# Seventeen hardware loops of a two-layer diffusion trunk written out as straight code

## The reference, cut to what matters

```python
for l in range(DEPTH):                       # DEPTH = 2
    need_ctx = l < DEPTH - 1
    mod = (sc @ w_mod[l] + b_mod[l]).reshape(B, 1, N_MOD, D)
    h = modulate(rms_norm(x, g_mix[l]), mod[:, :, 0], mod[:, :, 1])
    ...
    # token_mixer: retention, latent attention (MLA), grouped attention (GQA)
    z = (gs[:, :, 0] * (y_ret @ w_ret_o)
         + gs[:, :, 1] * (y_mla @ w_mla_o)
         + gs[:, :, 2] * (y_gqa @ w_gqa_o))
    y = z @ w_out
    x = x + mod[:, :, 2] * y
    h2 = modulate(rms_norm(x, g_ffn[l]), mod[:, :, 3], mod[:, :, 4])
    x = x + mod[:, :, 5] * ((silu(a) * b) @ w_ffn_out[l])   # a, b = split(h2 @ w_ffn_in[l])
return rms_norm(x, g_final)
```

## Time and profile before

| | |
|---|---|
| median of 3 runs | 3332.19 us (3330.65 to 3338.51) |
| the profiled execution's own time | 3329.75 us |
| its span, first to last instruction | 3327.9 us |
| mean granted TensorE clock over the span | 0.981 |
| PE busy | 3141.2 us (94%), 18376 matmuls |
| PEld busy | 2670.4 us (80%) |
| DVE busy | 1489.7 us (45%) |
| ACT busy | 1215.1 us (37%) |
| POOL busy | 399.5 us (12%) |
| DMA | 303.63 MB, mean 91 GB/s |

### The profile page before, as it was taken

The page is one execution under the profiler, slowest core; times in us unless marked ns, Lnnn a source line. Parts: engine busy times, 40 slices in busy tenths (PEclk is TensorE's granted clock), DMA queues, the critical chain, the costliest instruction groups (busy, mean ns, idle before and its releaser), DMA issues.

```text
span 3327.9 us, 46166 instructions
## 1 busy us (share of the span) xinstructions
PE 3141.2 (94%) x18376; PEld 2670.4 (80%) x18376; DVE 1489.7 (45%) x2073; ACT 1215.1 (37%) x1809; POOL 399.5 (12%) x304
## 2 busy tenths in 40 slices
PE   6899999999999999999999988999999999999998
PEld 5788888899888878788888867877788787778886
DVE  5455524445436634422222255554455456443334
ACT  3344433445434422311211234444355445332222
POOL 0011100111102201000100100111011112010101
PEclk9999999999999999999999989999999999999999
DMA  4111142111241243123132242112222232322232
GB/s 178 64 54 58 65 138 73 58 62 58 76 152 63 82 133 133 57 88 127 63 120 95 101 139 68 62 62 89 82 86 67 89 123 82 133 80 97 95 97 100
DMA packets 99807, 303.63 MB, mean 91 GB/s; under 512 B 10960, under 2 KB 23376, under 8 KB 99664
## 3 DMA queue, kind: packets, MB, share of 16 engines
q1 hardware_dynamic: 54720, 190.34, 16.9%
q10 hardware_dynamic: 44944, 111.32, 10.0%
HBM read 271.73 MB, written 29.88 MB: 91 GB/s over the span
## 4 chain that ended last, share of the span: by engine, by line
PE 79%; DVE 8%; issue 6%; ACT 4%; POOL 1%; DMA 1%; ACTq 1%; DVEq 0%; POOLq 0%
PE ps L1517 73%; PE ps L1605 2%; PE ps L1632 1%; DVE wl L980 1%; ACT wh L487 1%; POOL ptl L1499 1%; DVE tmp L985 1%; DVE ptl L1021 1%; DVE mx L1006 1%; DVE tmp L1153 1%; DVE hl L1162 1%; PE ps L1722 0%; PE ps L1575 0%; ACT pth L523 0%; ACT prob L535 0%
## 5 line engine op out<-in xcount | busy, mean ns | idle before, releaser
L1517 PE MATMUL ps<-hh,wh 128*128 128x512 f32 x2768 | 831.4, 360 | 41.3 <-DVE wl L980 20.2
L1517 PE MATMUL ps<-hl,wh 128*128 128x512 f32 x2768 | 813.4, 354 | 0.0
L1517 PE MATMUL ps<-hh,wl 128*128 128x512 f32 x2768 | 812.0, 353 | 0.0
L980 DVE TENSOR_TENSOR wl<-raw,wh 128x1024 fp32r<-128x1024 f32 (+2 forms) x356 | 465.5, 1308 | 523.1 <-ACT wh L487 509.9
L1517 PEld LDWEIGHTS ps<-hh,wh 128*128 128x128 f32 x2768 | 452.7, 190 | 125.0 <-issue 34.9
L1517 PEld LDWEIGHTS ps<-hh,wl 128*128 128x128 f32 x2768 | 452.2, 190 | 76.4
L1517 PEld LDWEIGHTS ps<-hl,wh 128*128 128x128 f32 x2768 | 453.1, 190 | 73.5 <-issue 0.7
L487 ACT ACTIVATE wh<-raw 128x1024 fp32r<-128x1024 f32 (+2 forms) x356 | 362.0, 1018 | 222.2 <-PE ps L1517 187.1
L1517 PE MATMUL ps<-yh,wh 128*128 128x512 f32 (+1 forms) x1296 | 405.9, 367 | 24.4 <-DVE wl L980 11.9
L1517 PE MATMUL ps<-yh,wl 128*128 128x512 f32 (+1 forms) x1296 | 393.9, 358 | 0.0
L1517 PE MATMUL ps<-yl,wh 128*128 128x512 f32 (+1 forms) x1296 | 393.7, 358 | 0.0
(11 more groups left out here) (212 smaller groups left out, 3312.4 us busy)
## 6 DMA issues: line engine op xcount, KB each, us to landing
raw<-in_stream SPq DMA_DIRECT2D x328, 512.0 KB, 3.2
prob<-in_wmod ACTq DMA_DIRECT2D x40, 512.0 KB, 3.2
mraw<-in_wmod ACTq DMA_DIRECT2D x36, 512.0 KB, 3.3
gspill<-prob ACTq DMA_DIRECT2D x32, 384.0 KB, 2.3
tmp<-gspill ACTq DMA_DIRECT2D x24, 384.0 KB, 3.2
early_y<-in_wmod SPq DMA_DIRECT2D x12, 512.0 KB, 14.2
vraw<-gspill ACTq DMA_DIRECT2D x16, 384.0 KB, 4.0
dec<-in_dec ACTq DMA_DIRECT2D x8, 768.0 KB, 4.2
```

The lines of the kernel that those rows point to most:

```text
L980: dve.tensor_tensor(wl[:, s, 0:n], raw[:, s, 0:n], wh[:, s, 0:n].bitcast(F32), ALU.subtract).then_inc(sem("w_lo"), 1)
L1517: ins = pe.matmul(out, lhs[w], rhs[x](cols), start=start and n == 0, stop=stop and n == 2)
```

## The change

Each of the seventeen `Fori` becomes a Python `for` over the same range, so that every turn is emitted with constants for its waits and addresses: five on ACT (merge, ret, two in out, ffn), five on DVE (the same), three on POOL (the sums in out, ret, ffn) and four on PE (merge, ret, out, ffn). The order of the work on each engine, the buffers and the semaphores stay as they are. The helpers `At.v`, `At.half` and `At.chunk` give the same numbers for a constant turn as for a register.

```diff
 merge, ACT
-                    with act.Fori(0 if ph["begun"] else 1, turns - 1) as i:
+                    for i in range(0 if ph["begun"] else 1, turns - 1):
 ret, ACT
-                    with act.Fori(0, turns - 1) as i:
+                    for i in range(0, turns - 1):
 out, ACT (both branches)
-                        with act.Fori(0, turns - 1) as i:
+                        for i in range(0, turns - 1):
 ffn, ACT
-                    with act.Fori(1 if ph["paired"] else 0, turns) as i:
+                    for i in range(1 if ph["paired"] else 0, turns):
 merge, DVE
-                    with dve.Fori(0 if ph["begun"] else 1, turns) as i:
+                    for i in range(0 if ph["begun"] else 1, turns):
 ret, DVE
-                    with dve.Fori(0, turns - 1) as i:
+                    for i in range(0, turns - 1):
 out, DVE (both branches)
-                        with dve.Fori(0, turns) as i:
+                        for i in range(0, turns):
-                        with dve.Fori(0, turns - 1) as i:
+                        for i in range(0, turns - 1):
 ffn, DVE
-                    with dve.Fori(1 if ph["paired"] else 0, turns) as i:
+                    for i in range(1 if ph["paired"] else 0, turns):
 out (sums), POOL
-                    with pool.Fori(0, turns - 1) as i:
+                    for i in range(0, turns - 1):
 ret, POOL; ffn, POOL
-                    with pool.Fori(0, turns) as i:
+                    for i in range(0, turns):
 merge, PE
-                    with pe.Fori(1, turns) as i:
+                    for i in range(1, turns):
 ret, PE; out, PE
-                    with pe.Fori(0, turns) as i:
+                    for i in range(0, turns):
 ffn, PE
-                    with pe.Fori(1 if ph["paired"] else 0, turns) as i:
+                    for i in range(1 if ph["paired"] else 0, turns):
```

## The result

The changed kernel takes 3315.56 us (median of 5 runs, 3310.99 to 3321.72) where the kernel before took 3334.18 us beside it: a ratio of 0.9941, 95% interval 0.9922 to 0.996. It is faster, by about the size that was forecast (3317.8 us). A second measurement gave 0.9961 (0.9947 to 0.9975). The profiled execution took 3310.99 us with a span of 3309.2 us, 18.8 us less than that of before; as will be seen, some of this difference belongs to the single execution and its clock.

The account below looks back on a forecast made before the run. PE, holding 79% of the chain of waits, was taken to bound the kernel; 5.85 + 1.7 + 3.6 + 3.3 = 14.4 us off the profiled 3329.75 gave 3315.3, so 3317.8 us for the median, range 3309 to 3328.

Parts of the forecast that it names:

- The entries: Four merges after the attentions: PE's waits shrink as ACT's table load and register work before the copy go; 5.85 us.
- Rival (1): Merge entries: table loads stay, inserted by a rule that doesn't see one history; 6.5 us missing, 3324.3 us; chance 0.11.
- rival (2): Merge entries: gain given back at the next wait, gate's load or stream late; 5.85 us missing, 3323.7 us; chance 0.10.
- The clock behind the second entry: After the second merge entry: the 3.42 us stretch at granted clock 0.50 goes with the shorter wait; 1.7 us.
- the clock low in new places: Sign that the prediction is wrong: low granted clock where there was none; a like stretch elsewhere would cost 1.7 us.
- Rival (3): Both `z` and the `out` after them: more low-clock stretches go, 1.7 us each; three make 3312.7 us; chance 0.13.
- The turn ends: First layer's feed-forward out loops: eleven turn ends with PE's branch and register work exposed, 0.33 us each; 3.6 us.
- The dependent steps: DVE and ACT chains PE waits for, at `z`, `out` and first merge folds: shorter gaps between dependent instructions; 3.3 us.
- Worth nothing: Retention, `ffn` loops, inner turns of merge and `out`, POOL's loops, SP's loads: no gain; PE's added code packets: 0 taken.
- Rival (4): New straight stretches: PE's code comes late, 1.1 us per packet boundary; all 60 give 3384 us; chance 0.04.

Follow-up runs that it names:

- the early sigmoid: Kernel before, all loops kept, plus a one-column sigmoid behind the last exponential of each attention: ratio 0.9974, 8.7 us less.
- the three parts that leave the entry alone: Kernel before with only PE's out loop written out (0.9986), only ret and ffn loops (0.9998), or merge on DVE, PE and out on ACT, DVE, POOL (0.9989).
- the part with ret and ffn: Kernel before with only the ret and ffn loops written out on ACT, DVE, POOL and PE (eight edits): ratio 0.9998.
- The parts: Four kernels, each the kernel before with a disjoint share of the seventeen edits: 7.7, 4.7, 0.7 and 3.7 us less.
- the part with ACT's merge loop: Kernel before with only ACT's merge loop written out: ratio 0.9977, 7.7 us of 3332.08.
- the moved high part: Changed kernel with the first high part of the four merges after the attentions moved ahead of ACT's DMA issues: 0.9945, then 0.9943 (3312.18 us).

## Why the prediction came out right, point by point

**The entries.** Forecast 5.85 us, measured 1.41 + 1.49 + 1.47 + 1.45 = 5.82 us, and the waits left, 0, 0.64, 0.26 and 1.17 us, were foretold as under 0.2, 0.5, 0.2 and 1.1 us. The cause holds as well: the experiment with the early sigmoid removes the load and keeps the loop. Rival (1) falls by L487's rows; rival (2) falls because the merges' whole stretches lose at least as much as their entries (the third entry and the 269 matmuls up to the next phase's first sum fall from 58.18 to 56.71 us, 1.47, which is what the entry itself lost).

**The clock behind the second entry.** At that place the forecast is right: the half-clock stretch of the earlier trace rows is there in both executions of before and in the three parts that leave the entry alone, and is missing in all nine executions in which the entry is shorter. The size fits there too: from the last matmul ahead of the entry to the end of the merge pass 71.6 and 72.0 us before and 68.4 to 68.8 after, 1.3 to 2.0 us less than the entry alone explains. But the wait is not the whole rule: behind the fourth entry, where the distance is longer (3.01 us), only two of the five executions that leave it alone show such a stretch. In the whole execution a single place can't be made out: the half-clock time is 105.8 us twice before, and 85.3, 105.8 and 109.2 after. What the step missed is that such stretches wander by more than the term. For the same reason "the clock low in new places", a sign of being wrong, can't be read: the places differ between two executions of one kernel. Rival (3), more clock at other waits, is borne out in part: at layer 2's `z` and the `out` behind it both executions of before have two half-clock stretches and all three of after have one, while behind layer 1's `z` the stretch stays.

**The turn ends.** Forecast 3.6 us, measured 3.56. The price that held is the difference of the two pairs, 0.33 us, in which the row of the taken branch has 0.208; by the Trainium skill's 0.108 us (Advanced Engine Details and Errata, Control Flow Timing) the term would have been 2.5 us, and the trace does not agree with it. What the step missed is that two of the eleven ends lead into `ffn`. There 0.62 us is saved, and the groups behind them run at the slow pace. That costs 2.48 us in the second group, and in the third 1.91 us against the one execution of before that had the fast pace there and nothing against the other.

**The dependent steps.** Forecast 3.3 us. The mechanism is right, several sizes were off. At the two `z` 0.55 and 0.3 us were forecast and 0.75 and 0.56 measured: PE's entry into `out` (0.27 us) belongs to both and was counted in one only, in part. The last out: 1.0 forecast, 1.1 measured at the seven distances, and 1.8 us over the whole phase, since the matmuls next to them come closer as well. Two ends of out gave 0.23 and 0.24 us as forecast; at the third the gain of 0.12 to 0.66 us stands beside longer waits of up to 1.0 us right after it, so nothing can be read. At the head of layer 2's first out 0.45 us can't be told from the landing of `xz`: its two waits together took 3.92 and 3.48 us before, 2.69, 3.14 and 4.17 us after. From the first folds of the merges to the next matmul pass 0.38 and 0.44 us in place of 0.48 and 0.47, 0.13 us together where 0.25 were forecast. Not foretold: the second modulation row in layer 1's last `out` comes after 0.40 to 0.51 us in place of 0.89 and 1.00.

**Worth nothing.** Right for retention, the inner turns of ffn, and the code: 147 packets where about 150 were forecast (49 more, where the estimate had 60), and no gap. The Trainium skill (Advanced Engine Details and Errata, ISA Cache) gives TensorE 128 KB for code. The 2.41 MB of packets agree with code that doesn't fit there and is fetched as it is reached. Rival (4), which made a stall of it, falls by the part with ret and ffn and by the whole.

**The sum.** 14.4 us were forecast. The parts give 16.8, the whole 19.7 and 13 in two measurements. The traces split it. The distances between matmuls that lie outside of the half-clock stretches of all five profiled executions add up to 3103.1 and 3103.3 us in the two executions of before and to 3090.7, 3093.6 and 3093.8 us in the three of after: 9 to 13 us, where the forecast had 12.7 without its clock term. There it lacked one loss (the pace, 2.5 to 4.4 us), and terms that came out higher (`z`, last out, modulation row, 1.7 us together) make up a part. The rest goes with the clock. The mean granted clock is 0.9822 in twelve timed executions of the changed kernel and 0.9805 in seventy of before (0.9822 and 0.9812 in the second measurement alone); 0.001 to 0.0017 of 3325 us is up to 3 to 6 us, more than the term of 1.7 us. What brings all of it no experiment shows: the part with ACT's merge loop, in which the stretch behind the second entry is gone, has 0.9803, and ret with ffn, which leaves the entries alone, 0.9814. So the large terms are right for their reasons, and that the total fits is in part luck: a loss that was left out and a clock that came out higher offset each other.

## What to carry to other kernels

A loop costs where its engine, or the engine that it releases, has just been waited for: price the entries, the turn ends behind a wait and the dependent steps one by one, and leave the covered turns alone. Look at what an activation's table history is at a loop's top: a load that is put there can be moved by one small activation in idle time, with the loop kept, and that gave as much as writing the loop out. When PE bounds the kernel, compare equal stretches of matmuls in number per time before and after: behind an edit a long group can run at another pace, 2% slower, and a saved gap is lost several times over. And look at the granted clock of every execution before two times are compared: in the runs of the changed kernel it lies between 0.980 and 0.984, and 0.004 of 3320 us is up to 13 us, as much as the change is worth.

## What the runs showed of the hardware that was not expected

- PE issues the same pairs of matmuls at two paces at full granted clock: three pairs of 512 and 256 columns in 1.04 or 1.06 us. A group keeps its pace to its last matmul (130.45 or 132.95 us, 102.09 or 100.17, and 114.06 or 116.25 us for 658 matmuls of the first group), in all fourteen profiled executions. What decides is open: the first group is slow in the part with ret and ffn, with the early sigmoid and with the moved high part alone, and in the third group two executions of the same kernel before differ.
- The stretches at a granted clock of 0.50 sum to between 85 and 116 us from 60 us on to 3290 us in the fourteen profiled executions. The times of three executions of one kernel follow them (85.3, 105.8, 109.2 us; 3310.99, 3318.38, 3322.3 us).
- A stretch at 0.50 of 3.42 us follows the second entry in all five executions with a distance of 2.41 us there and in none of the nine with a shorter one, and the fourth entry in two of the five with 3.01 us. So the length of the gap alone doesn't decide.
- A weight load of 512 KB for the modulation took 3.5 us until PE could start in the changed kernel and 5.3 us with PE's loop in ffn back, though PE came equally long after its issue and the neighbouring loads were issued at the same distances.
